# Spreading the 128-column blocks over all expert units, and evening out the turns of the unit transfers

## The reference, cut to what matters

```python
D_MODEL, SEQ, N_EXPERTS, TOP_K, D_FF_EXPERT = 1024, 256, 8, 2, 3584
def swiglu(x, w_gate, w_up, w_down):
    return (jax.nn.silu(x @ w_gate) * (x @ w_up)) @ w_down
def moe_swiglu(h, router_w, w_gate, w_up, w_down):
    xt = h.reshape(B * T, D)
    logits = (xt @ router_w).astype(jnp.float32)
    top_val, top_idx = lax.top_k(logits, TOP_K)
    gates = jax.nn.softmax(top_val, axis=-1)
    combine = jnp.einsum("nk,nke->ne", gates, jax.nn.one_hot(top_idx, N_EXPERTS, dtype=jnp.float32))
    y = jnp.zeros((B * T, D), dtype=jnp.float32)
    for e in range(N_EXPERTS):
        y = y + combine[:, e:e + 1] * swiglu(xt, w_gate[e], w_up[e], w_down[e]).astype(jnp.float32)
    return y.reshape(B, T, D).astype(h.dtype)
```

## Time and profile before

| what | us |
|---|---|
| median of 3 runs (1574.97 to 1576.73) | 1575.26 |
| the profiled execution, its own time | 1578.41 |
| its span, first to last instruction | 1576.6 |
| TensorE (PE) busy in it | 1511.0 |
| LDWEIGHTS (PEld) busy in it | 1306.0 |
| VectorE (DVE) busy in it | 253.9 |

### The profile page before, as it was taken

The page is one execution under the profiler, slowest core; times in us unless marked ns, Lnnn a source line. Parts: engine busy times, 40 slices in busy tenths (PEclk is TensorE's granted clock), DMA queues, the critical chain, the costliest instruction groups (busy, mean ns, idle before and its releaser), DMA issues.

```text
span 1576.6 us, 51984 instructions
## 1 busy us (share of the span) xinstructions
PE 1511.0 (96%) x24693; PEld 1306.0 (83%) x24693; DVE 253.9 (16%) x490; ACT 177.2 (11%) x383; POOL 143.3 (9%) x167
## 2 busy tenths in 40 slices
PE   9999999999999999999999999999999999999987
PEld 7786587777687864989999899999999999898886
DVE  3433310000143434100000100100100100100102
ACT  4123120000131332200000000000000000000001
POOL 2243200000022522200000000000000000000000
PEclk9999999999999999999999999999999999999999
DMA  9213344444243144999999999999999999999993
GB/s 342 90 49 134 107 161 160 160 160 148 80 174 107 55 158 188 358 387 388 373 367 373 365 362 384 357 363 371 370 377 379 365 380 368 364 373 379 384 391 142
DMA packets 133602, 433.31 MB, mean 275 GB/s; under 512 B 9082, under 2 KB 33916, under 8 KB 119052
## 3 DMA queue, kind: packets, MB, share of 16 engines
q1 hardware_dynamic: 132384, 427.69, 72.6%
q0 software_dynamic: 672, 2.14, 0.5%
q10 hardware_dynamic: 332, 0.13, 0.0%
HBM read 428.89 MB, written 1.05 MB: 273 GB/s over the span
## 4 chain that ended last, share of the span: by engine, by line
PE 93%; issue 3%; DVE 2%; ACT 1%; POOL 1%; DMA 0%; ACTq 0%; DVEq 0%
PE ps L1144 35%; PE ps L1179 18%; PE ps L1000 9%; PE ps L699 8%; PE ps L1011 4%; PE ps L862 4%; PE ps L710 3%; PE ps L1221 2%; PE ps L819 1%; PE ps L1080 1%; PE ps L732 1%; PE ps L829 1%; PE ps L695 1%; PE ps L725 1%; PE ps L839 1%
## 5 line engine op out<-in xcount | busy, mean ns | idle before, releaser
L1144 PE MATMUL ps<-wpost,ring 128*64 128x80 f32 (+1 forms) x5040 | 215.0, 237 | 8.6 <-issue 7.1
L1144 PE MATMUL ps<-AT_sb,ring 128*64 128x80 f32 x5104 | 211.9, 236 | 11.5 <-issue 11.4
L1144 PEld LDWEIGHTS ps<-AT_sb,ring 128*64 128x64 f32 x5104 | 205.1, 141 | 20.4 <-issue 17.6
L1144 PEld LDWEIGHTS ps<-wpost,ring 128*64 128x64 f32 (+1 forms) x5040 | 208.1, 142 | 16.5 <-issue 11.5
L1179 PEld LDWEIGHTS ps<-LT_sb,ring 128*64 128x64 f32 (+1 forms) x5104 | 203.9, 140 | 19.1 <-issue 15.4
L1179 PE MATMUL ps<-LT_sb,ring 128*64 128x80 f32 (+1 forms) x5104 | 210.9, 236 | 8.7 <-issue 7.9
L1000 PEld LDWEIGHTS ps<-hT_sb,ring 128*128 128x128 f32 x768 | 136.0, 190 | 24.6 <-issue 9.1
L1000 PE MATMUL ps<-hT_sb,ring 128*128 128x256 f32 (+1 forms) x768 | 155.7, 362 | 0.0
L699 PE MATMUL ps<-hT_sb,ring 128*128 128x256 f32 x576 | 128.2, 380 | 0.0
L699 PEld LDWEIGHTS ps<-hT_sb,ring 128*128 128x128 f32 x576 | 108.1, 190 | 15.0 <-DVE late L1657 0.5
L2008 POOL TENSOR_SCALAR small<-small 128x1 f32<-128x1 f32 x16 | 3.8, 240 | 1189.6 <-ACT late L1535 918.8
(11 more groups left out here) (285 smaller groups left out, 1097.7 us busy)
## 6 DMA issues: line engine op xcount, KB each, us to landing
ring<-in_moe_w_gate SPq DMA_DIRECT2D x84, 1024.0 KB, 8.4
ring<-in_moe_w_up SPq DMA_DIRECT2D x84, 1024.0 KB, 8.7
ring<-in_moe_w_down SPq DMA_DIRECT2D x84, 1024.0 KB, 8.5
late<-in_moe_w_up SPq DMA_DIRECT2D x28, 1024.0 KB, 8.1
late<-in_moe_w_gate SPq DMA_DIRECT2D x28, 1024.0 KB, 9.1
late<-in_moe_w_down SPq DMA_DIRECT2D x28, 1024.0 KB, 8.4
ring<-in_ffn_w_gate SPq DMA_DIRECT2D x11, 1024.0 KB, 5.4
ring<-in_ffn_w_up SPq DMA_DIRECT2D x11, 1024.0 KB, 8.1
```

Source lines behind the costliest of these rows:

```text
L1144: return mm(o[lo:lo + width, :], pairs[:, m % 2, lo:lo + width], xgT[e % 2][:, k, :], start=(k == 0 and m % 4 == 0), stop=(k == KD - 1), s ...
```

## The change

Every unit below 294 has one wide block, its last, and fifteen narrow ones (294 wide blocks, 10458 calls). The walk through TensorE's instructions counts one wait more at the start of an expert. Units are spread evenly over the turns up to three turns ahead of the last use, and where a turn would issue one unit beside a turn with two, the neighbour unit (never a down unit) is issued as two DMAs of 512 KB, one in each of the two turns. The semaphore targets follow the number of DMAs that a buffer gets.

```diff
-TURNS_AHEAD = 2
-UNITS_A_TURN = 2
+TURNS_AHEAD = 3
+WIDE_BLOCKS = 1
-WAITS = {"g0": 5, ...
+WAITS = {"g0": 6, ...
 def wide_blocks(n):
-    return UNIT_BLOCKS // 2 if n % 4 == 3 and n < LAST_WIDE else 0
+    return WIDE_BLOCKS if n < LAST_WIDE else 0
...
-    unit_turn = [max(free_at[i], 1 + i // UNITS_A_TURN) for i in range(ROUND_UNITS - N_UNIT)]
-    assert all(turn <= used_at[N_UNIT + i] - TURNS_AHEAD for i, turn in enumerate(unit_turn))
-    return set(turns), unit_turn
+    issues = ROUND_UNITS - N_UNIT
+    last = used_at[ROUND_UNITS - 1] - TURNS_AHEAD
+    unit_turn = [max(free_at[i], 1 + i * (last - 1) // (issues - 1)) for i in range(issues)]
+    part_turns = shared_turns(unit_turn, free_at)
+    for i, parts in enumerate(part_turns):
+        assert free_at[i] <= parts[0] and parts[-1] <= used_at[N_UNIT + i] - TURNS_AHEAD
+    return set(turns), part_turns
+
+def shared_turns(unit_turn, free_at):
+    kinds = [kind for kind, e, c, j in UNITS][N_UNIT:]
+    at_turn = {}
+    for i, turn in enumerate(unit_turn):
+        at_turn.setdefault(turn, []).append(i)
+    parts, taken = [(turn,) for turn in unit_turn], set()
+    for turn, units in at_turn.items():
+        if len(units) > 1 or turn in taken:
+            continue
+        for other, pick in ((turn + 1, 0), (turn - 1, -1)):
+            beside = at_turn.get(other, ())
+            if len(beside) == 2 and other not in taken and kinds[beside[pick]] != "d" \
+                    and free_at[beside[pick]] <= min(turn, other):
+                parts[beside[pick]] = min(turn, other), max(turn, other)
+                taken |= {turn, other}
+                break
+    return parts
+
+def landings():
+    counts, done = [], [0] * N_UNIT
+    for n in range(ROUND_UNITS):
+        done[n % N_UNIT] += 16 * len(PART_TURNS[n])
+        counts.append(done[n % N_UNIT])
+    return counts, done
...
-                        sp_.wait_ge(page_turn, UNIT_TURN[n - N_UNIT])
...
+                        rows = len(ks) // len(PART_TURNS[n])
+                        parts = [(dst[:, lo:lo + rows, :], src[:, lo:lo + rows, :]) for lo in range(0, len(ks), rows)]
-                    sp_.dma_start(dst, src).then_inc(unit_landed[n % N_UNIT], 16)
+                    for turn, (to, of) in zip(PART_TURNS[n], parts):
+                        if first and n >= N_UNIT:
+                            sp_.wait_ge(page_turn, turn)
+                        sp_.dma_start(to, of).then_inc(unit_landed[n % N_UNIT], 16)
...
-                    wide = wide_blocks(n) // len(ks)
-                    for k in ks:
-                        if kind == "g" and c == 0 and k % 4 == 0:
+                    narrow = UNIT_BLOCKS - wide_blocks(n)
+                    for i, (k, m) in enumerate(itertools.product(ks, range(MOE_TILES[c]))):
+                        if kind == "g" and c == 0 and k % 4 == 0 and m == 0:
                             pe.wait_ge(xg_ready, per_round(r, 2 * e + k // 4 + 1, 2 * N_EXP))
-                        for m in range(wide, MOE_TILES[c]):
-                            for lo in (0, P // 2):
-                                ins = block(k, m, lo, P // 2)
-                                turned(ins, e, f"{kind}{c}", call)
-                                call += 1
-                    for k in ks:
-                        for m in range(wide):
-                            ins = block(k, m, 0, P)
+                        for lo in (0, P // 2) if i < narrow else (0,):
+                            ins = block(k, m, lo, P // 2 if i < narrow else P)
                             turned(ins, e, f"{kind}{c}", call)
                             call += 1
```

More of the change, by code:

```diff
@@ L17 @@
+import itertools
 from contextlib import ExitStack
@@ L105 @@
 TURN_MARKS = (8,)
-TURNS_AHEAD = 2
-UNITS_A_TURN = 2
+TURNS_AHEAD = 3
 UNIT_BLOCKS = 16
+WIDE_BLOCKS = 1
 LAST_WIDE = ROUND_UNITS * (N_EXP - 1) // N_EXP
-WAITS = {"g0": 5, "u0": 1, "g1": 2, "d0": 2, "u1": 1, "g2": 2, "gather": 2, "d1": 1, "u2": 1, "g3": 2, "d2": 1,
+WAITS = {"g0": 6, "u0": 1, "g1": 2, "d0": 2, "u1": 1, "g2": 2, "gather": 2, "d1": 1, "u2": 1, "g3": 2, "d2": 1,
          "u3": 1, "d3": 1, "y": 2, "s0": 1}
 def wide_blocks(n):
-    return UNIT_BLOCKS // 2 if n % 4 == 3 and n < LAST_WIDE else 0
+    return WIDE_BLOCKS if n < LAST_WIDE else 0
 def unit_calls(n):
@@ L174, in page_turns @@
                     call += 1
-    unit_turn = [max(free_at[i], 1 + i // UNITS_A_TURN) for i in range(ROUND_UNITS - N_UNIT)]
-    assert all(turn <= used_at[N_UNIT + i] - TURNS_AHEAD for i, turn in enumerate(unit_turn))
-    return set(turns), unit_turn
-PAGE_TURNS, UNIT_TURN = page_turns()
+    issues = ROUND_UNITS - N_UNIT
[28 more added lines that the diff above has]
+    return counts, done
+PAGE_TURNS, SHARED = page_turns()
+PART_TURNS = [(None,)] * N_UNIT + SHARED
+UNIT_LANDED, LANDED_A_ROUND = landings()
 assert ROUND_UNITS % N_UNIT == 0
@@ L610, in moe_loads @@
                         lo = (MOE_AT[c] + 2 * j) * P
-                        dst = unit_of(n)
-                        src = moe_down[0, e][lo:lo + 2 * P, :].rearrange("(p i) d -> p (i d)", p=P)
+                        parts = [(unit_of(n), moe_down[0, e][lo:lo + 2 * P, :].rearrange("(p i) d -> p (i d)", p=P))]
                     else:
@@ L1125, in landed @@
             def landed(r, n):
-                pe.wait_ge(unit_landed[n % N_UNIT], per_round(r, 16 * (n // N_UNIT + 1), 16 * ROUND_UNITS // N_UNIT))
+                pe.wait_ge(unit_landed[n % N_UNIT], per_round(r, UNIT_LANDED[n], LANDED_A_ROUND[n % N_UNIT]))
             def m_in(r, kind, e, c, part=None):
@@ L1180, in block @@
                                   start=(first and m % 4 == 0), stop=last, skip_group_check=True)
[L1182 to L1191, removed]
+                    narrow = UNIT_BLOCKS - wide_blocks(n)
+                    for at, (i, m) in enumerate(itertools.product(range(2), range(KD))):
+                        for lo in (0, P // 2) if at < narrow else (0,):
+                            ins = block(i, m, lo, P // 2 if at < narrow else P)
                             turned(ins, e, f"d{c}", call)
```

## The result

The changed kernel takes 1585.22 us (median of 7 runs, 1579.81 to 1590.42) against 1574.97 for the kernel before (7 runs beside it, 1571.41 to 1576.73). The ratio is 1.0064, with a 95% interval of 1.0043 to 1.0086: slower by 0.6%, where 1554 us, 1.4% faster, had been forecast. The profiled execution took 1582.53 us, with a span of 1580.7.

What follows compares the result with a forecast made beforehand. PE mostly bounds the part with wide blocks, transfers the last expert. Wide part 783, last expert 98 and tail 18.5 make 899.6 us, 21.5 less than the stage's 921.1, so 1575.3 becomes 1553.8; range 1540 to 1571.

Steps and rivals of the forecast that it cites:

- What bounds the kernel: Expert stage: the part with wide blocks is mostly bound by PE (5.69 us a turn), the last expert by transfers (5.45).
- Blocks: Expert units: 290 wide blocks become narrow pairs, each gaining 0.10 us, so 29 us less work of PE.
- a rival with s: Entering and leaving wide mode costs s us a switch; slower from 0.26, total about 1615 at 0.39; chance 0.05.
- ten starts at an even 0.121 us: Run of eight wide blocks: ten matmuls start in 1.21 us, leaving hardly anything for the entry into wide mode.
- More instructions: PE's instruction stream: 1167 more instructions, 4.6 pages, giving 168 turns and 5.13 us of PE work a wide-part page.
- Evenness: Wide-part pages: every page takes about 5.1 us, below the 5.45 its transfers need, so the backlog should never empty.
- Turns: Turns of one and a half units: backlog up to 5.45 us covers the missing 1.0 us, costed at nothing.
- the case without cover: Turns of one and a half units: without backlog cover each would lose 1.0 us, at most 14.
- the page-floor rival: Instruction fetch: a page costs 5.45 us whatever was issued; 1566, or 1580 by the straight line; chance 0.18.
- The halves and three turns ahead: Unit issue: halves costed at nothing, perhaps a few us worse by the skill's table; three turns ahead gains nothing.
- a fetch that passes freely: Fetch in its own queue would not wait for backlog, giving the full-speed rival's 1542 us; that rival's chance 0.14.

Runs made afterwards that it cites:

- runs of four: Changed kernel with its lone wide blocks gathered four together in every fourth unit (292 blocks), same turns: 1574.12 us, ratio 1.0000 to the kernel before.

## Why the prediction was wrong, point by point

**What bounds the kernel: right.** PE in the wide part, transfers by way of page fetches in the last expert. The half-byte runs show both sides: the fetch stalls go with the bytes, and 54 us of the kernel before are the transfers' doing.

**Blocks: the step that failed.** "I take 0.24 and a gain of 0.10 us a block" put one price on a wide call wherever it stands. 0.24 is what a further block in a run costs (0.235 measured); each run costs 0.31 us on top, so a lone one is 0.545, and a block in a run of eight 0.274, more than the 0.228 to 0.24 read from the chain. Then 294 lone blocks cost 160 us, and the 584 in 73 runs of eight cost 160 too: the change removes nothing on the wide side, and 290 pairs at 0.138 us add 40. The runs with half the bytes measured 38. The rows had bounded this (a run holds up to 0.78 us that could be the switch), and I had priced it as a rival with s and dismissed it with ten starts at an even 0.121 us. Those ten were the last of sixteen matmuls and said nothing of how the run began or of what starts after it. The measured s is 0.31 us, above the rival's deciding point of 0.26: 221 x 0.31 is 69 us more, against the 29 saved, again 40. The rival on the slower side was the right mechanism, at a chance of 0.05. Its sum, with 0.31, would have given about 1600 us instead of 1585, because it kept the stalls of before on top of the longer work.

**Why only 10 us of the 38 show.** The kernel before had stalls that the longer work absorbs: 25.6 us of waits for "issue" from 640 to 1400 in the kernel before become 4.0 in the changed one. The rest of the 28 us lies in late starts within the busy time (19 us of it in the kernel before, 10 in the changed one, by the runs with half the bytes). In all the transfers cost the kernel before 54 us and the changed one 27. Work that is added beside a stalled fetch is paid only as far as it exceeds the stall.

**More instructions: the count was right** (168 turns, 53162 instructions against 51984), and it matters only together with the blocks.

**Evenness: right as to stalls, not as a gain.** The pages became more even, but longer than the 5.1 us expected: half of the turns came 5.36 to 5.95 us apart, where in the kernel before half came 5.08 to 6.13 apart. So PE stayed busy and the transfers, not PE, went idle.

**Turns: the cover was mis-sized.** "The up to 5.45 us of backlog covers the missing 1.0" failed. With PE's work as forecast (runs of four), turns of less than two units cost about 2.2 us each by the stretches, 15 us, just above the 14 that I had named for the case without cover. So even if a lone block had cost what the forecast said, the forecast would have been 20 us low (1554 against the 1574 of runs of four); the page-floor rival's 1566 to 1580 held for that kernel, though the half-byte run shows its reason (a floor per page) to be wrong. What is queued at a page start has to be small, or the next fetch is late; that it must also bridge the time until the new units' packets flow is my reading of the standstill, and was not tested by itself. The forecast's other premise, that with shorter pages the backlog never empties, fell with it.

**The halves and three turns ahead**: nothing, as costed. The Trainium skill's advice of at least 1 MiB ("DMA: Bandwidth & Descriptors", Bandwidth, Measured) could be neither confirmed nor contradicted by seven halved units; the changed kernel with and without them is the same within the intervals.

**The fetch and the queues.** The Trainium skill ("DMA: Bandwidth & Descriptors", Arbitration) has each DMA engine take its queues in turn, packet by packet. I had read it as a fetch that passes freely, and the runs rule that out: without wide blocks the time fell from 1582.8 to 1449.2 us when only the bytes were halved. But the same sentence says that an engine finishes a whole packet, of typically 9 to 17 descriptors, before it changes queues, and with that the runs are compatible. One engine's share of a 1 MiB unit is 64 KB, sixteen of the 4 KB pieces that the trace records, and 2.8 us at 371 GB/s for the sixteen engines (an estimate). The fetch starts a median of 2.3 us after SP's first issue of a turn in the kernel before and 0.3 us before it with half the bytes, so the queued units delay it by 2.6 us, about one such share and far less than the 8.4 us of backlog that the prediction had named. What the engines take as one packet in this kernel was not tested.

## What to carry to other kernels

The mean price of an instruction in a run of its kind is not its price alone between others: before such instructions are spread out, find the price of the first one, or bound it by the whole surplus of a run, and let that bound carry weight in the forecast. Take such prices from start to start, up to a point behind the run where the starts are regular again; the length of a row in the chain leaves out what the next instruction waits. Where instruction fetches and bulk transfers share the DMAs, time the same kernel with half the bytes: it separates the engine's own work from what the transfers hold up, in one run. Added work hides in the stalls it displaces, and saved work is lost in them, so near such a balance a change of one of the two shows only in part.

## What the runs showed of the hardware

A change between calls of 64 and of 128 columns has a price. For a float32 block of 128 x 128 against 80 columns, two narrow calls take 0.138 us; one wide call takes 0.235 in the middle of a run, and each run of one to sixteen costs 0.31 on top. About half of that falls at the way in (the first wide matmul starts 0.16 us after the last narrow one instead of 0.063, the second 0.18 after the first instead of 0.118) and half at the way out (0.21 to the first narrow pair, then 0.12 to the second).

The fetch of one 16 KB page depends on what is queued, and it ends the stalls at page starts: in the kernel before, the 29 stalls of over 0.3 us between 650 and 1400 us end a median of 2.44 us after the start of the instruction packet before them (the middle half 2.40 to 2.50), and the 83 of the kernel without wide blocks 2.40 (2.34 to 2.48). The packet itself takes 1 us with all bytes and with half. In the kernel before, the page that begins at 1524.08 us sees the next page's packet only after 1527; the queues of 1527 to 1528 us:

```profile
q1 hardware_dynamic: 129, 0.37, 101.8%
q8 instruction: 1, 0.02, 6.5%
```

There is none in 1524 to 1527, and the stall ends at 1529.58. With half the bytes one stall of 0.2 us is left in the kernel without wide blocks and none in the other two.
